# A low-rank product in fp32 column tiles from the unnormalised input, and the decay products two value blocks later

## The chip, the cores and the metric

The kernel runs on one core of one Trainium2 chip. The metric is its device time in microseconds, the median of several executions. The core has TensorE (PE: matmul, and PEld: its weight loads), VectorE (DVE), ScalarE (ACT), GpSimd (POOL) and SyncE (SP), which issues DMAs. Each engine works through its own instructions in order and waits on semaphores for the others.

## What is computed

Two transformer-like blocks on 512 tokens of width 1024, in fp32: the first with a recurrent layer, an attention layer and two MLPs, the second with gated linear attention (GLA), a pooling branch and a gated MLP. The change lies at the seam: the end of the first block's second MLP, its last norm, and the first projections of the second block.

```
x = rms_norm(x, final_norm_g)                 # end of the first block
h = rmsnorm(x, norm_mix)                      # second block
q, k, v, r, lr_f, lr_b, u, g_a, g_b = split(h @ w_in)      # lr_f, lr_b: 16 columns each
log_a_f = log_sigmoid(lr_f @ w_decay_up_fwd + b_decay_fwd) / 16
log_a_b = log_sigmoid(lr_b @ w_decay_up_bwd + b_decay_bwd) / 16
b = cumsum(log_a)   (in chunks of 64 tokens)
q_e, k_e, k_d = q * exp(b), k * exp(-b), k * exp(b_last - b)
scores = mask(q_e @ k_e^T);  o = scores @ v + q_e @ state;  kv = k_d^T @ v
```

There are 4 heads; q and k have 128 columns a head, v has 256.

## The kernel before

**Data.** The activations stand turned, as X: 8 chunks k of 128 features, each 128 x 512 tokens, in fp32. For the large products an operand is split into a high part (rounded to fp32r) and a low part (the rest): Ahi and Alo are X times the norm weights gfm, split so. A product of 128 output features (helper `product`, with `three`) runs over 8 chunks, three fp32r matmuls each (lines 1023 to 1025: hi by hi, hi by lo, lo by hi), 24 matmuls of 512 tokens in all. The tokens' reciprocal roots are not in Ahi: they come from a separate sum of squares and are multiplied in as a result leaves its bank (`scale_out`, line 2105).

**Weights.** They come in units of 8 chunks x 256 columns. SyncE loads a unit into one of two stages, ScalarE rounds it into whi (`hi`, line 1500), and VectorE takes the difference into wlo (`lo`, line 2093). `take_unit` makes TensorE wait for the latter. Both engines do this at fixed places between their other steps. The unit "lr" holds the 32 low-rank columns three times beside each other. It and K0 use the same slot of whi and wlo, Q0 and V0 the other; then V1 uses K0's, and Q1 V0's.

**PSUM.** Six banks go round as a ring in the order of the labels added to it: `begin` waits until the bank's last user has been read. Banks 6 and 7 are apart.

**The order of TensorE** is written by hand. After the last turned sums of the MLP (line 1160) it runs: the low-rank product lr (96 columns) and qk 0 beside each other chunk by chunk (`first_products`, in the order TURN = 4, 5, 6, 7, 0, 1, 2, 3, as Ahi and Alo become ready); qk 2; qk 1 (unit K0); the two root sums over the squares (fp32 with ones, lines 1330 and 1331); qk 3; the values of head 0 (unit V0) in four blocks of 128 tokens, 24 matmuls of 256 columns each, with the decay products z (line 1339) behind the first; the values of head 1 (V1); the scores and turned keys of head 0 (lines 1359 and 1059); qk 4 and qk 6 (unit Q1), and so on: states (1375), r 0, outputs (1385, 1393).

**The others around it.** ScalarE squares each chunk twice (line 1819), and splits K0's hi between the fourth and the fifth pair. GpSimd and VectorE sum the squares (938, 2601); VectorE takes K0's lo behind its third sum. Then come V0's split and the roots; the reciprocal (2611); lr scaled and split into lr3 by rows (high, low, high parts in the three copies, against the same of wdec); the scaling of qk 0 to 3; V1's split. The decays of head 0 go from z through Abs, Exp and Ln on ScalarE (1842, 1845, 1848), two scans on VectorE, Exp (1854) and products for the scaled queries and keys. Behind that chain, in ScalarE's order, stand the copies of V of head 0 out of its banks (1871, 1873) and the hi of Q1; in VectorE's stands Q1's lo. After it follow on VectorE a reciprocal, eight steps on X, the masked scores, R0's lo and the scaling of qk 4.

Of the kernel before, what the change touches and what calls it, by code (L numbers as in the profile page):

```python
# [9 lines left out]
ALU = mybir.AluOpType  # L10
# [77 lines left out]
def program(nc, I, out, scratch):  # L88
# [62 lines left out]
    ysum = const("ysum", [128, 8])  # L151
    dec = at("dec", o_const + 4 * KB + 512, [128, 2, 8])
# [96 lines left out]
    unit("lr", *[wpiece(win, 0, 8, 3072, 32, 32 * i) for i in range(3)])  # L249
# [174 lines left out]
    pair("lr", "lr")  # L424
    ring.add(("qk", 0))
    pair(("Q", 0), ("qk", 2))
    pair(("K", 0), ("qk", 1), ("qk", 3))
    ring.add(("v", 0, 0), ("z", 0, 0), ("z", 0, 1))
    pair(("V", 0), ("v", 0, 1))
# [156 lines left out]
    V = pool("V", 16, [128, 4, 4, 256])  # L586
    lr, lr3 = pool("lr", 96, [96, S]), pool("lr3", 32, [96, S], R)
    CM = pool("CM", 34, [128, 8, 64])
    wdec, wdec3 = pool("wdec", 102, [96, 2, 512]), pool("wdec3", 36, [96, 2, 512], R)
    SR = pool("SR", 48, [128, 8, S])  # L590
# [420 lines left out]
    def tensor_program(e):  # L1011
# [25 lines left out]
        def first_products(fill, *parts):  # L1037


            for i, k in enumerate(TURN):  # L1040
                e.wait_ge(s_alo, FILL[fill] + i + 1)
                for label, s, c0_, width in parts:
                    ps = begin(label) if i == 0 else ring.bank(label)
                    t = three(ps[0:width, :], hi_of(s)[:, k, c0_:c0_ + width], lo_of(s)[:, k, c0_:c0_ + width], Ahi[:, k, :], Alo[:, k, :], i == 0, i == 7)
                    if i == 7:
                        t.then_inc(*ring.put(label))
# [274 lines left out]

        s = take_unit("lr")
        first_products("gla", ("lr", s, 0, 96), (("qk", 0), take_unit(("Q", 0)), 0, 128))
        s = u_of["Q", 0]
        product(("qk", 2), s, 128, Ahi, Alo)
        s = take_unit(("K", 0))
        product(("qk", 1), s, 0, Ahi, Alo)
        e.wait_ge(s_tsp, 7)
# [3 lines left out]
        product(("qk", 3), s, 128, Ahi, Alo)  # L1332
# [8 lines left out]
        def values(h, behind_first=None):  # L1341
            s = take_unit(("V", h))
            for jj in range(2):
                ps = begin(("v", h, jj))
                for j in (2 * jj, 2 * jj + 1):
                    for k in range(8):
                        t = three(ps[:, (j % 2) * 256:(j % 2 + 1) * 256], Ahi[:, k, j * 128:(j + 1) * 128], Alo[:, k, j * 128:(j + 1) * 128],
                                  hi_of(s)[:, k, :], lo_of(s)[:, k, :], k == 0, k == 7)
                    if j == 0 and behind_first:
                        behind_first()  # L1350
                t.then_inc(*ring.put(("v", h, jj)))
# [130 lines left out]
    def scalar_program(e):  # L1482
        st = Steps(s_act)

        def hi(u):
# [14 lines left out]
            e.activation(hi_of(u)[:, 0:nk, 0:n], source(u), ACT.Copy).then_inc(s_hi, 1)  # L1500
# [310 lines left out]
        def for_gla(n, m):  # L1811
# [3 lines left out]
            for n, m in enumerate(TURN):  # L1815
                for i, (acc, t, kw) in enumerate(((sqa_e, sqt_e, {}), (sqb_e, sqs_e, {"scale": c1("fin1", m)}))):
                    if n > 2:
                        e.wait_ge((s_tsp, s_ssr)[i], n - 2)
                    e.activation((t[n % 2] if n else acc)[:, :], X[:, m, :], ACT.Square, **kw).then_inc(s_tsa, 1)
                if n == 3:  # L1820
                    hi(u_of["K", 0])
# [263 lines left out]
    def vector_program(e):  # L2085
        st = Steps(s_dve)

        def lo(u):
# [3 lines left out]
            e.wait_ge(s_hi, u + 1)  # L2092
            e.tensor_tensor(lo_of(u)[:, 0:nk, 0:n], source(u), f32(hi_of(u)[:, 0:nk, 0:n]), ALU.subtract).then_inc(s_lo[slot_of[u]], 1)  # L2093
# [499 lines left out]
        e.tensor_tensor(gfm[:, :], c1("fin1", 0, 8), c2("mix2", 0, 8), ALU.mult).then_inc(*st.inc())  # L2593
        mlp(1, lambda n, m: scaled_lo("gla", m, gfm[:, m:m + 1], n))
# [379 lines left out]
```

## Time and profile before

| | us |
|---|---|
| median of 3 runs | 1801.88 |
| lowest, highest | 1801.77, 1803.03 |
| the profiled execution | 1804.51 |
| its span, first to last instruction | 1803.3 |

The profile is of one execution. Its page gives the busy time of each engine and the costliest groups, its timeline the instructions in order of time, its stretches the busy time between two moments with the granted clock of TensorE (1.00 is 2.4 GHz). A matmul's record is longer than its share of the pipeline: full products follow each other every 0.23 us with records of 0.39, so the starts are to be read. An fp32 matmul leaves two records, and rows of one kind may be merged.

### The profile page before, as it was taken

What the parts mean: (1) busy time and instruction counts of PE and PEld (TensorE: products, weight loads), DVE (VectorE), ACT (ScalarE), POOL (GpSimd) and SP (SyncE); (2) the same over time, 40 slices, a digit from 0 to 9 for tenths busy, and PEclk for the clock granted to TensorE, in tenths of its full rate; (3) what the DMA queues carried; (4) which work ended last, traced back from release to release, by engine and by line L of the source; (5) the groups of instructions that cost most, each with busy time, mean ns of one, the idle gap of its engine ahead of it and who ended that gap; (6) DMA issues with size and microseconds to landing.
All of it is one profiled execution on the core that took longest, in us unless ns stands there. A gap on an engine that the chain in (4) does not pass through costs nothing.

```text
span 1803.3 us, 21912 instructions
## 1 busy us (share of the span) xinstructions
PE 1787.6 (99%) x8577; PEld 1458.5 (81%) x8577; DVE 1270.5 (70%) x1680; ACT 813.0 (45%) x1072; POOL 305.8 (17%) x246
## 2 busy tenths in 40 slices
PE   9999999999999999999999999999999999999998
PEld 7888888888877668888888878888888888888886
DVE  7896868686879865767686888666446555846757
ACT  6753534343444862444343455566323343323334
POOL 0004000000145874000000041111012311011012
PEclk9999999999999999999999999999999999999999
DMA  7233253443234003452525232222332323431512
GB/s 235 94 117 117 71 187 83 130 130 102 65 100 136 29 1 117 131 173 47 167 59 172 44 110 76 66 71 71 103 107 83 104 83 140 140 117 48 175 59 76
DMA packets 153350, 186.39 MB, mean 103 GB/s; under 512 B 8704, under 2 KB 121472, under 8 KB 153248
## 3 DMA queue, kind: packets, MB, share of 16 engines
q1 hardware_dynamic: 144944, 166.13, 28.4%
q0 software_dynamic: 7760, 18.35, 4.9%
q8 instruction: 68, 1.11, 0.2%
q10 hardware_dynamic: 544, 0.52, 0.1%
q14 instruction: 34, 0.28, 0.0%
HBM read 182.71 MB, written 2.14 MB: 103 GB/s over the span
## 4 chain that ended last, share of the span: by engine, by line
PE 86%; DVE 7%; ACT 3%; POOL 2%; issue 1%; DMA 1%; SPq 0%; DVEq 0%; POOLq 0%; ACTq 0%
PE bank L1023 27%; PE bank L1024 26%; PE bank L1025 26%; PE bank L1244 1%; PE bank L1059 1%; DVE work L2495 1%; PE bank L1270 1%; DVE t L2492 1%; DVE XC L2190 1%; PE bank L1375 1%; ACT whi L1500 1%; DVE wlo L2093 1%; PE bank L1393 1%; PE bank L1248 1%; DVE work L2470 0%
## 5 line engine op out<-in xcount | busy, mean ns | idle before, releaser
L1023 PE MATMUL bank<-Ahi,whi 128*128 128x512 f32 (+1 forms) x1400 | 549.2, 392 | 0.8 <-DVE wlo L2119 0.5
L1025 PE MATMUL bank<-Ahi,wlo 128*128 128x512 f32 (+1 forms) x1400 | 544.0, 389 | 0.0
L1024 PE MATMUL bank<-Alo,whi 128*128 128x512 f32 (+1 forms) x1400 | 544.0, 389 | 0.0
L2093 DVE TENSOR_TENSOR wlo<-stage,whi 128x2048 fp32r<-128x2048 f32 (+1 forms) x133 | 304.9, 2293 | 174.3 <-ACT whi L1500 174.1
L1500 ACT ACTIVATE whi<-stage 128x2048 fp32r<-128x2048 f32 (+1 forms) x139 | 262.6, 1889 | 189.3 <-PE bank L1025 157.3
L1023 PEld LDWEIGHTS bank<-Ahi,whi 128*128 128x128 f32 x1400 | 262.8, 188 | 62.8 <-issue 8.2
L1025 PEld LDWEIGHTS bank<-Ahi,wlo 128*128 128x128 f32 x1400 | 262.7, 188 | 54.6
L1024 PEld LDWEIGHTS bank<-Alo,whi 128*128 128x128 f32 x1400 | 263.0, 188 | 54.0 <-issue 1.2
L1023 PE MATMUL bank<-whi,Hh 128*128 128x512 f32 x602 | 234.8, 390 | 0.0
L1025 PE MATMUL bank<-whi,Hl 128*128 128x512 f32 x602 | 234.2, 389 | 0.0
L1024 PE MATMUL bank<-wlo,Hh 128*128 128x512 f32 x602 | 234.2, 389 | 0.0
L1023 PEld LDWEIGHTS bank<-whi,Hh 128*128 128x128 f32 x602 | 113.0, 188 | 24.5 <-DVE wlo L2093 0.6
L1025 PEld LDWEIGHTS bank<-whi,Hl 128*128 128x128 f32 x602 | 113.0, 188 | 23.5
L1024 PEld LDWEIGHTS bank<-wlo,Hh 128*128 128x128 f32 x602 | 113.0, 188 | 23.3
L1650 ACT ACTIVATE Hw<-ht 128x512 f32<-128x512 f32 x64 | 40.5, 633 | 201.2 <-DVE ht L2295 201.2
L2093 DVE TENSOR_TENSOR wlo<-quad,whi 128x2048 fp32r<-128x2048 f32 (+1 forms) x44 | 98.6, 2241 | 30.1 <-ACT whi L1500 30.1
L1500 ACT ACTIVATE whi<-quad 128x2048 fp32r<-128x2048 f32 (+1 forms) x44 | 82.3, 1871 | 72.7 <-DVE quad L2336 49.2
L816 POOL DMA_DIRECT2D quad<-in_mlp_w_down x8 | 10.5, 1316 | 535.8 <-DVE quad L2336 498.5
L2356 DVE TENSOR_TENSOR D<-D,bank 128x512 f32<-128x512 f32 x138 | 90.4, 682 | 14.3 <-PE bank L1025 14.1
L2295 DVE SCALAR_TENSOR_TENSOR ht<-bank,rstd 128x512 f32<-128x512 f32 x64 | 44.0, 688 | 62.2 <-PE bank L1025 61.2
L1002 POOL TENSOR_TENSOR Hw<-fu,fg 128x512 f32<-128x512 f32 x22 | 28.4, 1291 | 286.4 <-DVE fu L2851 286.4
L926 POOL TENSOR_SCALAR pt<-pt,stat 128x128 f32<-128x128 f32 (+3 forms) x60 | 63.3, 1066 | 14.4 <-DVE stat L2532 13.6
(364 smaller groups left out, 2491.3 us busy)
## 6 DMA issues: line engine op xcount, KB each, us to landing
stage<-in_mlp_w_up SPq DMA_DIRECT2D x32, 1024.0 KB, 5.3
stage<-in_w_in SPq DMA_DIRECT2D x22, 1024.0 KB, 5.1
stage<-in_w_ffn_in SPq DMA_DIRECT2D x22, 1024.0 KB, 4.9
quad<-in_mlp_w_down SPq DMA_DIRECT2D x16, 1024.0 KB, 6.6
stage<-in_mlp_w_down SPq DMA_DIRECT2D x16, 1024.0 KB, 5.1
quad<-in_mlp_w_down POOLq DMA_DIRECT2D x8, 1024.0 KB, 8.6
stage<-in_rec_w_in SPq DMA_DIRECT2D x6, 1024.0 KB, 5.2
stage<-in_att_w_in SPq DMA_DIRECT2D x6, 1024.0 KB, 5.1
```

The costliest lines, as they stand in the source:

```text
L926: e.tensor_scalar(p, p, stat[:, i % 8, 2:3], None, ALU.mult).then_inc(s_p, 1)
L1002: e.tensor_tensor(to, fu[n % 2][:, :].rearrange("p (a t) -> p a t", a=2), fg[n % 4][:, :].rearrange("p (a t) -> p a t", a=2), ALU.mult).th ...
L1023: e.matmul(ps, hi, rh, start=first, stop=False, skip_group_check=onto)
L1024: e.matmul(ps, hi, rl, start=False, stop=False, skip_group_check=onto)
L1025: return e.matmul(ps, lo, rh, start=False, stop=last, skip_group_check=onto)
L1059: t = e.transpose(ps[:, i * 128:(i + 1) * 128], part, ident_[:, :])
L1244: x = e.matmul(ps[:, 0:nk], QT[p0:p0 + 64, h // 2, j * 128:(j + 1) * 128], KT[p0:p0 + 64, h // 2, 0:nk], start=True, stop=not j)
L1500: e.activation(hi_of(u)[:, 0:nk, 0:n], source(u), ACT.Copy).then_inc(s_hi, 1)
L1650: e.activation(to, x, ACT.Square).then_inc(s_q, 1)
L2093: e.tensor_tensor(lo_of(u)[:, 0:nk, 0:n], source(u), f32(hi_of(u)[:, 0:nk, 0:n]), ALU.subtract).then_inc(s_lo[slot_of[u]], 1)
L2295: e.scalar_tensor_tensor(ht[n % 8][:, :], ring.bank(label)[:, :], 0.0, rstd[:, :], ALU.max, ALU.mult).then_inc(*ring.take(label))
L2356: e.tensor_tensor(to, to, ps[:, :], ALU.add if SIGN[r] > 0 else ALU.subtract).then_inc(*done)
```

## The change

The unit "lr" is loaded once, 32 columns. ScalarE copies it, unrounded, into low_w, which lies where whi of its slot lies, and VectorE multiplies it there by gfm. A constant sel (128 x 96: four identities of 32 above each other, three times beside each other) is made on VectorE before the second MLP.

TensorE multiplies low_w with the raw X in plain fp32: 8 matmuls of 32 columns, one a chunk, in two groups of four. Chunk k writes partitions 32 (k mod 4) on of the bank "lrp", so four chunks go to four column tiles; the second group adds to the first. The first group stands before, the second in the middle of the first products, which now are qk 0 and qk 2. ScalarE copies lrp to SBUF (lrs) behind its second pair of squares. The matmul sel by lrs adds the four parts and lays the sum out three times, as "lr" was; its place is behind the root sums, which themselves now stand behind qk 3. The decay products z stand behind the third value block of head 0. The ring's order follows, with one label more.

```diff
-    unit("lr", *[wpiece(win, 0, 8, 3072, 32, 32 * i) for i in range(3)])
+    unit("lr", wpiece(win, 0, 8, 3072, 32))
...
-    pair("lr", "lr")
-    ring.add(("qk", 0))
-    pair(("Q", 0), ("qk", 2))
+    pair("lr", "lrp")
+    pair(("Q", 0), ("qk", 0), ("qk", 2))
     pair(("K", 0), ("qk", 1), ("qk", 3))
-    ring.add(("v", 0, 0), ("z", 0, 0), ("z", 0, 1))
-    pair(("V", 0), ("v", 0, 1))
+    ring.add("lr")
+    pair(("V", 0), ("v", 0, 0), ("v", 0, 1))
+    ring.add(("z", 0, 0), ("z", 0, 1))
...
+                if i == 4 and between:
+                    between()
...
-        s = take_unit("lr")
-        first_products("gla", ("lr", s, 0, 96), (("qk", 0), take_unit(("Q", 0)), 0, 128))
-        s = u_of["Q", 0]
-        product(("qk", 2), s, 128, Ahi, Alo)
+        take_unit("lr")
+        low_ps = begin("lrp")
+        def low_rank(*ks):
+            for k in ks:
+                e.wait_ge(*ring.free(("xt", 1, k)))
+                row = k % 4 * 32
+                t = e.matmul(low_ps[row:row + 32, :], low_w[:, k, 0:32], X[:, k, :], start=k >= 4, stop=k < 4)
+            if ks[-1] == TURN[-1]:
+                t.then_inc(*ring.put("lrp"))
+        low_rank(*TURN[:4])
+        s = take_unit(("Q", 0))
+        first_products("gla", (("qk", 0), s, 0, 128), (("qk", 2), s, 128, 128), between=lambda: low_rank(*TURN[4:]))
         s = take_unit(("K", 0))
         product(("qk", 1), s, 0, Ahi, Alo)
+        product(("qk", 3), s, 128, Ahi, Alo)
...
-        product(("qk", 3), s, 128, Ahi, Alo)
+        ps = begin("lr")
+        e.wait_ge(*ring.free("lrp"))
+        e.matmul(ps[0:96, :], sel[:, :], lrs[:, :], start=True, stop=True).then_inc(*ring.put("lr"))
...
-                    if j == 0 and behind_first:
-                        behind_first()
+                    if j == 2 and behind_third:
+                        behind_third()
...
+                if n == 1:
+                    e.wait_ge(*ring.full("lrp"))
+                    e.activation(lrs[:, :], ring.bank("lrp")[:, :], ACT.Copy).then_inc(*ring.take("lrp"))
                 if n == 3:
                     hi(u_of["K", 0])
...
+                e.tensor_tensor(low_w[:, :, :], low_w[:, :, :], gfm[:, :].unsqueeze(2).broadcast_to([128, nk, n]), ALU.mult).then_inc(s_lo[slot_of[u]], 1)
```

TensorE at the start of the second block's products, before. whi_55 is the slot of "lr" and later of K0, whi_54 that of Q0; D are the MLP's sums that are turned:

```order
L1160 MATMUL bank<-ident_64,D_101 128x128 [waits s_free3]
L1023 MATMUL bank<-Ahi_50,whi_55 96x512 [waits s_alo,s_free0,s_lo0,s_lo1]
L1024 MATMUL bank<-Alo_51,whi_55 96x512
L1025 MATMUL bank<-Ahi_50,wlo_58 96x512
L1023 MATMUL bank<-Ahi_50,whi_54 128x512 [waits s_free1]
L1024 MATMUL bank<-Alo_51,whi_54 128x512
```

The same place now:

```order
L1166 MATMUL bank<-ident_64,D_102 128x128 [waits s_free3]
L1337 MATMUL bank<-X_49,low_w_198 32x512 [waits s_free4,s_free0,s_lo1]
L1337 MATMUL bank<-X_49,low_w_198 32x512 [waits s_free5]
L1337 MATMUL bank<-X_49,low_w_198 32x512 [waits s_free0]
L1337 MATMUL bank<-X_49,low_w_198 32x512 [waits s_free1]
L1027 MATMUL bank<-Ahi_50,whi_54 128x512 [waits s_free1,s_alo,s_lo0]
```

Of each chunk's six matmuls the three of 96 columns have gone from between those of Q0, and four of 32 columns stand ahead.

TensorE from the end of qk 3 to the values of head 0, where before the root sums stood ahead of qk 3:

```order
L1029 MATMUL bank<-Ahi_50,wlo_58 128x512
L1349 MATMUL bank<-sq_e_92,ones_66 128x512 [waits s_ssr_and_decay_low,s_tsp]
L1350 MATMUL bank<-sq_e_93,ones_66 128x512
L1353 MATMUL bank<-lrs_204,sel_80 96x512 [waits s_free0,s_free5]
L1027 MATMUL bank<-whi_54,Ahi_50 128x256 [waits s_free0,s_lo0]
```

Three fp32 products now stand between qk 3 and the values.

ScalarE from the copy of lrp to the hi of K0, now (whi_55 from stage_53 is K0's hi):

```order
L1845 ACTIVATE lrs_204<-bank 128x512 [waits s_full0]
L1842 ACTIVATE sq_e_91<-X_49 128x512
L1842 ACTIVATE sq_e_94<-X_49,cols_69 128x512
L1842 ACTIVATE sq_e_95<-X_49 128x512 [waits s_tsp]
L1842 ACTIVATE sq_e_96<-X_49,cols_69 128x512 [waits s_ssr_and_decay_low]
L1523 ACTIVATE whi_55<-stage_53 128x2048 [waits s_full0,s_load1]
```

The first of these rows is new; the squares and K0's hi follow it as they were.

## Rows read from the trace of the kernel before

**Rows 1.** The page, part 1: engine, busy us (share) and instructions.
```profile
PE 1787.6 (99%) x8577; PEld 1458.5 (81%) x8577; DVE 1270.5 (70%) x1680; ACT 813.0 (45%) x1072; POOL 305.8 (17%) x246
```

**Rows 2.** Timeline, TensorE: start, us, line, operation; "x" counts merged records.
```profile
1050.06 0.48 PE L1023 MATMUL bank<-Ahi,whi 128*96 128x512 f32 x1
...
1072.47 1.10 PE L1330 MATMUL bank<-sq_e,ones 128*128 128x512 f32 x2
1073.40 1.02 PE L1331 MATMUL bank<-sq_e,ones 128*128 128x512 f32 x2
...
1079.73 0.28 PE L1023 MATMUL bank<-whi,Ahi 128*128 128x256 f32 x1
...
1082.71 0.70 PE L1339 MATMUL bank<-lr,wdec 96*128 96x512 f32 x2
...
1103.41 1.95 PE L1359 MATMUL bank<-qe,ke 128*128 128x128 f32 x16
...
1105.98 0.47 PE L1023 MATMUL bank<-Ahi,whi 128*128 128x512 f32 x1
...
1119.13 0.50 PE L1023 MATMUL bank<-Ahi,whi 128*128 128x512 f32 x1
```

**Rows 3.** By stretch: length, busy us as in rows 1, clock, DMA share, GB/s.
```profile
1050.06:1061.27 11.21, 11.21 (x52) 8.48 (x50) 9.00 (x12) 8.32 (x14) 3.90 (x4) 1.00 0.39 113
1061.27:1066.73 5.46, 5.46 (x26) 4.50 (x24) 5.36 (x4) 3.77 (x6) 4.81 (x2) 1.00 0.03 3
...
1079.73:1082.71 2.98, 2.98 (x25) 2.85 (x24) 2.88 (x6) 1.98 (x2) 2.23 (x4) 1.00 0.02 0
```

**Rows 4.** Timeline, VectorE: sums of squares, then the lo of K0.
```profile
1058.60 4.70 DVE L2601 TENSOR_TENSOR sq_e<-sq_e,sq_e 128x512 f32<-128x512 f32 x3 [1.45 <-ACT sq_e L1819]
1063.22 2.28 DVE L2093 TENSOR_TENSOR wlo<-stage,whi 128x2048 fp32r<-128x2048 f32 x1
```

**Rows 5.** Timeline, VectorE: the lo of Q1.
```profile
1101.71 2.29 DVE L2093 TENSOR_TENSOR wlo<-stage,whi 128x2048 fp32r<-128x2048 f32 x1 [4.24 <-ACT whi L1500]
```

**Rows 6.** Timeline, TensorE: full-width products, 64-column ones, the next product.
```profile
1132.34 1.89 PE L1385 MATMUL bank<-V,sc_t 128*128 128x256 f32 x8
1134.16 3.24 PE L1393 MATMUL bank<-ST,qe 128*64 128x256 f32 x28
1137.34 0.50 PE L1023 MATMUL bank<-Ahi,whi 128*128 128x512 f32 x1
```

**Rows 7.** Timeline, ScalarE: the second pair of squares, and the hi of K0.
```profile
1057.86 0.71 ACT L1819 ACTIVATE sq_e<-X,cols 128x512 f32<-128x512 f32 x1
...
1060.82 1.92 ACT L1500 ACTIVATE whi<-stage 128x2048 fp32r<-128x2048 f32 x1
```

**Rows 8.** Timeline, VectorE: reciprocal, QK 0 and 2, lo of V1, QK 4 and 6.
```profile
1076.62 3.35 DVE L2611 RECIPROCAL rstd<-sq_e 128x512 f32<-128x512 f32 x1 [0.70 <-ACT sq_e L1832]
...
1080.62 1.27 DVE L2105 TENSOR_TENSOR QK<-bank,rstd 128x512 f32<-128x512 f32 x2
...
1084.93 2.23 DVE L2093 TENSOR_TENSOR wlo<-stage,whi 128x2048 fp32r<-128x2048 f32 x1
...
1116.60 1.28 DVE L2105 TENSOR_TENSOR QK<-bank,rstd 128x512 f32<-128x512 f32 x2
```

**Rows 9.** Timeline, ScalarE: Abs of z, end of v 0 0, hi of Q1.
```profile
1083.22 1.26 ACT L1842 ACTIVATE t<-bank,negb 128x512 f32<-128x512 f32 x2
...
1098.54 0.47 ACT L1873 ACTIVATE V<-bank,rtok 128x256 f32<-128x256 f32 x1
...
1099.78 1.90 ACT L1500 ACTIVATE whi<-stage 128x2048 fp32r<-128x2048 f32 x1
```

**Rows 10.** Busy time by stretch, around 520 us, as in rows 3.
```profile
518.00:520.00 2.00, 1.55 (x8) 1.38 (x8) 0.00 (x0) 0.30 (x1) 2.00 (x1) 0.50 0.00 0
...
526.00:528.00 2.00, 2.00 (x14) 2.00 (x13) 1.09 (x3) 0.00 (x0) 0.00 (x0) 1.00 0.00 0
```

**Rows 11.** Timeline, TensorE, around 518 us.
```profile
518.45 2.14 PE L1197 MATMUL bank<-kk,qi 64*128 64x256 f32 x8 [1.32 <-DMA kk<-kk]
```

More of the change, by code:

```diff
@@ L151, in program @@
     ysum = const("ysum", [128, 8])
+    sel = const("sel", [128, 96])
+    assert c_at[0] <= o_const + 4 * KB + 512
     dec = at("dec", o_const + 4 * KB + 512, [128, 2, 8])
@@ L586, in program @@
     V = pool("V", 16, [128, 4, 4, 256])
+    low_w = at("low_w", o_whi + slot_of[u_of["lr"]] * 8 * KB, [128, 8, 32])
     lr, lr3 = pool("lr", 96, [96, S]), pool("lr3", 32, [96, S], R)
@@ L589, in program @@
     wdec, wdec3 = pool("wdec", 102, [96, 2, 512]), pool("wdec3", 36, [96, 2, 512], R)
+    lrs = pool("lrs", 56, [128, S])
     SR = pool("SR", 48, [128, 8, S])
@@ L1035, in product, with first_products @@
             i.then_inc(*ring.put(label))
-        def first_products(fill, *parts):
+        def first_products(fill, *parts, between=None):
             for i, k in enumerate(TURN):
+                if i == 4 and between:
+                    between()
                 e.wait_ge(s_alo, FILL[fill] + i + 1)
@@ L1339, in decays, with values @@
                 e.matmul(ps[:, :], wdec3[:, d, h * 128:(h + 1) * 128], lr3[:, :], start=True, stop=True).then_inc(*ring.put(("z", h, d)))
-        def values(h, behind_first=None):
+        def values(h, behind_third=None):
             s = take_unit(("V", h))
@@ L1499, in hi @@
                 e.wait_ge(*used(behind[u]))
-            e.activation(hi_of(u)[:, 0:nk, 0:n], source(u), ACT.Copy).then_inc(s_hi, 1)
+            to = low_w[:, :, :] if u == u_of["lr"] else hi_of(u)[:, 0:nk, 0:n]
+            e.activation(to, source(u), ACT.Copy).then_inc(s_hi, 1)
         def scaled_hi(m, gc):
@@ L2092, in lo @@
             e.wait_ge(s_hi, u + 1)
+            if u == u_of["lr"]:
+                e.wait_ge(*gfm_there)
+                e.tensor_tensor(low_w[:, :, :], low_w[:, :, :], gfm[:, :].unsqueeze(2).broadcast_to([128, nk, n]), ALU.mult).then_inc(s_lo[slot_of[u]], 1)
+                return
             e.tensor_tensor(lo_of(u)[:, 0:nk, 0:n], source(u), f32(hi_of(u)[:, 0:nk, 0:n]), ALU.subtract).then_inc(s_lo[slot_of[u]], 1)
@@ L2593, in vector_program @@
         e.tensor_tensor(gfm[:, :], c1("fin1", 0, 8), c2("mix2", 0, 8), ALU.mult).then_inc(*st.inc())
+        gfm_there = st.now()
+        e.tensor_tensor(sel[:, 32:96], ident[:, 0:64], ident[:, 64:128], ALU.add).then_inc(*st.inc())
+        e.wait_ge(*st.now())
+        e.tensor_tensor(sel[:, 0:32], sel[:, 32:64], sel[:, 64:96], ALU.add).then_inc(*st.inc())
+        e.wait_ge(*st.now())
+        for i in (1, 2):
+            e.tensor_copy(sel[:, 32 * i:32 * i + 32], sel[:, 0:32]).then_inc(*st.inc())
         mlp(1, lambda n, m: scaled_lo("gla", m, gfm[:, m:m + 1], n))
```

## The prediction

> **What bounds the kernel now.** The page's first part comes first: TensorE is busy for 1787.6 us, 99% of the span [rows 1]. So a microsecond counts only if TensorE gets it or waits for it, and the argument is about the 70 us in which the second block's first projections run. There I read TensorE's timeline for the starts of its stages [rows 2], the stretches between them for the price of a product [rows 3], and ScalarE's and VectorE's timelines for when each thing that TensorE needs is ready. What the reader is to see: TensorE hardly waits here, but two of its supplies arrive with little to spare. The split of weight unit K0 (hi on ScalarE, lo on VectorE) ends at 1063.22 + 2.28 = 1065.50 [rows 4], and TensorE takes it 72 products after 1050.06, at 11.21 + 5.46 us, 1066.73 [rows 2, 3]: slack 1.2 us. The split of Q1 ends at 1101.71 + 2.29 = 1104.00 [rows 5] and is taken at 1105.98 [rows 2]: slack 2.0 us. Q1's split stands on both engines behind the whole chain that the decay product z starts. The change shortens TensorE's way to the first and moves z nearer to the second.
>
> **The removed product.** The low-rank product is 24 products of 96 columns. Before, 48 interleaved ones take 11.21 us and 24 of qk 2 take 5.46 [rows 3]; after, qk 0 and qk 2 are the 48 interleaved ones, so 5.46 us go.
>
> **The added products.** Eight fp32 products of 32 columns on the raw X, in two groups of four. One fp32 product of 512 takes 0.93 us, from the start of line 1330 to that of line 1331 [rows 2]. Four column tiles beside each other are not in this trace, so I bound them: one after another 8 x 0.93 = 7.4 us, fully beside each other 2 x 0.93 = 1.9. Nearest are the 14 fp32 products of 64 columns of line 1393 (two records each): 3.18 us from their start to the next product, 0.23 us each, where the 4 of full width on line 1385 take 1.82 / 4 = 0.455 each [rows 6]. Two tiles do run beside each other, at twice the rate and with different moving operands. I take 1.0 us a group, 2.0 in all. The product after them starts a tenth of a microsecond late [rows 6], which is in that. The adding product with sel is one more fp32 product of 512: 0.93 us. By work alone: -5.46 + 2.0 + 0.93 = -2.5 us. The four small steps that make sel, and load, hi and scaling of low_w, lie on VectorE, SyncE and ScalarE well ahead of need, hidden by the second layer's last products: nothing.
>
> **First wait: K0.** TensorE wants K0 at 1050.06 + 1.0 + 5.6 + 1.0 + 5.6 = 1063.3 now. The split isn't earlier, it is later: on ScalarE the new copy of lrp stands behind the second pair of squares (start 1057.86 [rows 7]; the second group ends near 1057.9, so the copy waits for nothing) and costs 0.6 us, a copy of that size. So K0's hi starts at 1061.4 instead of 1060.82 and ends at 1063.3 [rows 7]. VectorE's three sums, 4.70 us from 1058.60 [rows 4], are fed by those squares and end near 1063.6; K0's lo then runs to 1065.85. TensorE stands still for 2.5 us, and qk 1 starts at 1065.9 instead of 1066.73. Behind it nothing of the 2.5 us gained is left but 0.8. The groups could cost 2.5 us more and this start would hardly move.
>
> **To the first value block.** 48 products by 5.46 / 24 make 10.9: 1076.8. The two root sums are no longer ahead of qk 3 but behind it. Before, they start at 1072.47 [rows 2]. Now they start at 1076.8, +4.4 us; with sel, 3 x 0.93 = 2.8 us, the values start at 1079.65, where they started at 1079.73: -0.1 us. What is new is that all that hangs on the root is 4.4 us late: the reciprocal ends at 1076.62 + 3.35 + 4.4 = 1084.35 instead of 1079.97 [rows 8]. QK 0 is scaled behind lr (0.6 us) and frees its bank at about 1085.7. By the new ring of banks the second half of the values (v 0 1) takes just that bank, and TensorE is there after two blocks, 2 x 2.88 = 5.76 us (a block is the stretch of 2.98 [rows 3] less the tenth in which z waits), at 1085.4: 0.3 us of waiting. The split of V1, from 1084.93 [rows 8], comes 4.4 us later too, ending near 1091.5; it is taken at 1092.0, so it is just hidden.
>
> **Second wait: the decays.** z was issued behind one value block, at 1082.71 [rows 2]; now it is behind three: 1079.65 + 8.64 + 0.3 = 1088.6, 5.9 us later. From z a chain leads through ScalarE and VectorE without slack: Abs at 1083.22, Exp, Ln, the scans, the factors, then V 0's two halves scaled and freed (the first half's second copy starts at 1098.54), hi of Q1 at 1099.78 [rows 9], lo of Q1 until 1104.00 [rows 5]; 21.3 us from z to split. All of it moves by 5.9 us. TensorE's own work moves by 0.1: it would be at the scores at 1103.55. Two things are late there. First, the scores' first bank is now the one of v 0 0, freed at 1098.54 + 0.47 + 5.9 = 1104.9: 1.4 us of waiting. Then the scores and the turned keys take 1105.98 - 1103.41 = 2.6 us [rows 2], to 1107.6, and Q1's split ends at 1104.00 + 5.9 = 1109.9: 2.4 us. qk 4 starts at 1110.0 instead of 1105.98, +4.0 us. The size doesn't hang on the first of these two, since the second ends last.
>
> **What follows.** VectorE is 5.9 us late and TensorE 4.0. QK 4 is scaled from 1116.60 [rows 8], so its bank is free at 1117.2 + 5.9 = 1123.1; the product r 0, at 1119.13 [rows 2] + 4.0 = 1123.1, takes it: at most 0.1 us more. From there VectorE waits for TensorE again, and TensorE is gap-free, so the 4 us stay to the end. Sum: -2.5 (work) + 2.5 (K0) + 0.3 + 1.4 + 2.4 (banks, Q1) - 0.1 = +4.0 us. The execution profiled took 1804.51 us for a span of 1803.3; it was 2.6 us above the median of 1801.88, and 1808.5 would be its counterpart. Against the median: **1805.9 us**. With half a microsecond to either side for K0's split, for z's chain and for the noise of the runs, its own range is 1804.7 to 1807.3.
>
> **Rival 1: the clock falls.** Ahead of 518 us TensorE did small transposes, one fp32 product and then waited 1.32 us at 518.45; the stretch from 518 has a granted clock of 0.50, 1.2 GHz, and at 526 it is 1.00 again [rows 10, 11]. Two places after the change look similar: 2.5 us of standing at 1063, and 1.4 and 2.4 us around short work at 1103 to 1110. For it: that row. Against: around both places stand full products, where ahead of 518 us there were hardly any. The low clock lasted about 7 us, with products at half rate: +3.4 us on +4.0, 1809.3 us. The Trainium skill (TensorE: Matmul & The Clock Gate, Part 1) says that inactivity throttles the array and activity releases it; by that rule this is what a long enough wait does, and [rows 10] agree.
>
> **Rival 2: the four tiles don't overlap.** Then a group takes 3.7 us. The second ends near 1063.2, ScalarE's copy waits for it, and squares, sums and both steps of K0 follow: split at about 1070.9, 5 us behind my 1065.9. All behind moves by that: 1810.9 us. Against it: the rate of line 1393 [rows 6]. The Trainium skill (TensorEngine Tiling, Key Properties) says that a change of tiling mode drains the array; the product at 1137.34 takes 0.50 us [rows 6], a small drain, and it would lie in front of K0's wait anyway.
>
> **Rival 3, not slower: K0 is there in time.** If the squares and sums give K0's split by 1063.3 (VectorE's sums take 1.6 us each beside GpSimd's own; alone they could be shorter), the root starts at 1074.2, z at 1086.0, and Q1's split at 1107.3 ends the wait: +1.4, 1803.3 us, within 0.2%. It decides from 1.0 us on: if K0 comes at 1064.9, the total is 1804.9. Against: hi of K0 can't end before 1063.3 by ScalarE's own order [rows 7], so lo can't before 1065.5. The same size of result comes if z's chain has slack that I don't see.
>
> **Rival 4, faster: neither wait is there.** The gain of 2.5 stays: 1799.3 us. It needs the chain from z to Q1 to shrink from 21.3 to 17.5 us or less [rows 2, 5]; nothing in it is idle long enough.
>
> **How the numbers follow.** Forecast 0.58, rival 1 0.14, rival 2 and other ways to lose more 0.07, rival 3 and its kin (from 1801.5 to 1804.7) 0.18, rival 4 0.03. The range from 1802.3 to 1809.6 leaves out rival 4, the low end of rival 3 and rival 2, some 0.15. 0.2%, about what a measurement can tell from no change, is 3.6 us: the border lies at 1805.5, inside the forecast's own range, whose upper two thirds lie above it (0.38). Slower: 0.38 + 0.14 + 0.07 = 0.59; within: 0.20 + 0.18 = 0.38; faster: 0.03.
>
> **What would show it.** K0: qk 1's first product waits for VectorE's wlo, some 2.5 us, and starts 0.8 us earlier than before relative to the stage's start. The groups: eight 32-column products with group starts 0.9 to 1.1 us apart. Values start where they did. z 5.9 us later. qk 4's first product waits for wlo, and the scores for ScalarE's V. If qk 4 starts less than 2 us later than before, the second wait is wrong; if the stage before K0 shows no gap, the first is. A granted clock under 1.00 at 1063 to 1073 or 1107 to 1117 speaks for rival 1. The forecast fails if K0's split ends ahead of 1064.9, or if the stage loses or regains time behind 1123.

## The result, and the profile after

| | before | after |
|---|---|---|
| median of 13 runs each, us | 1802.95 | 1808.21 |
| lowest, highest | 1801.57, 1804.89 | 1805.88, 1809.98 |
| the profiled execution | 1804.51 | 1807.09 |
| its span | 1803.3 | 1805.9 |

After takes 1.003 of before's time, 95% interval 1.0023 to 1.0037: +5.3 us, slower. The range from 1802.3 to 1809.6 us and the likeliest sign of the prediction hold; its forecast was +4.0 us. As an absolute time 1808.21 us lies above the forecast's own range, which ended at 1807.3; before's median over these 13 runs is itself 1.1 us above the 1801.88 that the forecast started from.

The spans differ by 2.6 us only, because of something far ahead of the change: around 518 us before's profiled execution has the low clock of [rows 10], and after's has not. This stretch of after answers to [rows 10]; the columns are length, busy us of PE, PEld, DVE, ACT and POOL, granted clock, DMA share and GB/s:

```profile
518.00:520.00 2.00, 1.47 (x10) 1.14 (x11) 0.00 (x0) 0.64 (x2) 2.00 (x1) 1.00 0.00 0
```

Of the twelve kernels traced here six have a low clock there and six have not, some built on before and some on after in each half. In one series of 27 runs of before, the 11 with a mean granted clock of 0.999 took 1801.20 to 1802.05 us and the 10 with 0.997 took 1804.14 to 1805.10. So I compare traces from the last work in front of the change that they share, the 13 turned sums of the MLP, to the end of the span. TensorE's timeline of before has them here (start, us, line, operation; in brackets the idle time ahead and who ended it):

```profile
1048.66 1.64 PE L1160 MATMUL bank<-ident,D 128*128 128x128 f32 x13 [0.58 <-DVE D L2356]
```

From there before takes 1803.3 - 1048.66 = 754.6 us. After starts them at 1045.83 and takes 1805.9 - 1045.83 = 760.1: **+5.4 us since the turned sums**, which is what the medians say too. All experiments below are given in that unit as well. It is read from one execution of each kernel, so where the medians say something else, that is given too. TensorE's last product of all, in before, in after and in the kernel before with only z moved (an experiment below):

```profile
1795.45 0.39 PE L1025 MATMUL bank<-whi,Hl 128*128 128x512 f32 x1
```
```profile
1797.72 0.39 PE L1029 MATMUL bank<-whi,Hl 128*128 128x512 f32 x1
```
```profile
1798.27 0.39 PE L1025 MATMUL bank<-whi,Hl 128*128 128x512 f32 x1
```

It starts 1795.45 - 1048.66 = 746.79 us after the turned sums in before, 751.89 in after: on TensorE the loss is 5.1 us. The other 0.3 lie behind its last product, where the last norms and writes take 8.18 us instead of 7.85. This end takes 7.5 to 7.9 us in the traces of the three kernels built on before and 8.1 to 8.2 in the nine built on after; why is open.

TensorE's timeline of after, with the rows that answer to [rows 2], and the waits:

```profile
1045.83 1.64 PE L1166 MATMUL bank<-ident,D 128*128 128x128 f32 x13 [0.59 <-DVE D L2386]
1047.40 1.07 PE L1337 MATMUL bank<-X,low_w 128*32 128x512 f32 x8
...
1054.28 1.07 PE L1337 MATMUL bank<-X,low_w 128*32 128x512 f32 x8
1055.28 0.50 PE L1027 MATMUL bank<-Ahi,whi 128*128 128x512 f32 x1
...
1062.72 0.50 PE L1027 MATMUL bank<-Ahi,whi 128*128 128x512 f32 x1 [1.70 <-DVE wlo L2123]
...
1073.73 1.02 PE L1349 MATMUL bank<-sq_e,ones 128*128 128x512 f32 x2
1074.59 1.02 PE L1350 MATMUL bank<-sq_e,ones 128*128 128x512 f32 x2
1075.45 1.02 PE L1353 MATMUL bank<-lrs,sel 128*96 128x512 f32 x2
...
1082.43 0.39 PE L1027 MATMUL bank<-whi,Ahi 128*128 128x256 f32 x1 [0.22 <-DVE QK L2135]
...
1085.40 0.63 PE L1361 MATMUL bank<-lr,wdec 96*128 96x512 f32 x2
...
1101.69 2.05 PE L1381 MATMUL bank<-qe,ke 128*128 128x128 f32 x16 [1.27 <-ACT V L1899]
1103.57 1.04 PE L1065 MATMUL bank<-ident,t 128*128 128x128 f32 x8
1106.68 0.60 PE L1027 MATMUL bank<-Ahi,whi 128*128 128x512 f32 x1 [2.07 <-DVE wlo L2123]
1107.08 0.63 PE L1028 MATMUL bank<-Alo,whi 128*128 128x512 f32 x1
1107.51 0.63 PE L1029 MATMUL bank<-Ahi,wlo 128*128 128x512 f32 x1
...
1121.43 0.50 PE L1027 MATMUL bank<-Ahi,whi 128*128 128x512 f32 x1
```

The reader sees the four waits that the prediction named, at the places it named: on VectorE's wlo for qk 1 (K0's split), on a scaled QK for v 0 1, on ScalarE's V for the scores, on wlo again for qk 4 (Q1's split). A group of four 32-column products takes 1.00 us (1054.28 to 1055.28). And a fifth thing stands at the end: behind qk 4's first product the next ones follow 0.40 to 0.43 us apart with records of 0.63, not 0.23 apart. The stretches of after show why, in the clock behind POOL's column:

```profile
1100.00:1106.68 6.68, 3.34 (x28) 2.90 (x26) 2.44 (x3) 6.42 (x12) 2.46 (x2) 1.00 0.01 1
1106.68:1110.00 3.32, 3.32 (x8) 2.61 (x9) 3.28 (x2) 2.14 (x2) 0.00 (x0) 0.54 0.64 182
1110.00:1119.38 9.38, 9.38 (x41) 7.46 (x39) 9.28 (x18) 0.00 (x0) 0.00 (x0) 0.98 0.14 49
```

TensorE is busy for 3.34 of 6.68 us up to qk 4; then for some 3.4 us it is granted 1.2 instead of 2.4 GHz, and does in them the work of 1.7. Behind K0's wait, with full products on both sides, the clock stayed at 1.00:

```profile
1062.00:1073.00 11.00, 10.28 (x45) 8.54 (x46) 9.37 (x6) 5.86 (x7) 10.37 (x7) 1.00 0.34 99
```

On VectorE's timeline the three sums of squares and K0's lo, the rows that answer to [rows 4], and on ScalarE's the copy of lrp and K0's hi:

```profile
1055.77 1.28 DVE L2638 TENSOR_TENSOR sq_e<-sq_e,sq_e 128x512 f32<-128x512 f32 x1 [1.44 <-ACT sq_e L1842]
1057.38 3.08 DVE L2638 TENSOR_TENSOR sq_e<-sq_e,sq_e 128x512 f32<-128x512 f32 x2 [0.34 <-ACT sq_e L1842]
1060.39 2.28 DVE L2123 TENSOR_TENSOR wlo<-stage,whi 128x2048 fp32r<-128x2048 f32 x1
```
```profile
1055.64 0.57 ACT L1845 ACTIVATE lrs<-bank 128x512 f32<-128x512 f32 x1
...
1058.39 1.90 ACT L1523 ACTIVATE whi<-stage 128x2048 fp32r<-128x2048 f32 x1
```

Lo starts 1060.39 - 1055.77 = 4.62 us behind the first sum, in before 1063.22 - 1058.60 = 4.62 [rows 4]. Hi ends at 1060.29, just ahead of lo, where before it ended at 1062.74 [rows 7], half a microsecond ahead: the copy has taken the slack that hi had, and has cost lo nothing. The later squares did reach VectorE, which stands 0.34 us behind its first sum; but that first sum took 1.28 us, where in before the three take 4.62 / 3 = 1.54 each. TensorE is busy for 1785.2 us, 2.4 less than in [rows 1], in a span that is longer from the change on:

```profile
PE 1785.2 (99%) x8571; PEld 1454.7 (81%) x8571; DVE 1270.4 (70%) x1684; ACT 812.7 (45%) x1073; POOL 305.5 (17%) x246
```

### The profile page after: what moved, and what is told of

The parts are those of the page before. It is cut to its first block, busy times and chain, and to the rows that moved or that the text cites. A ratio compares the mean times of both kernels' runs of the same rounds, so it can differ in the third digit from the quotient of the medians.

```text
span 1805.9 us, 21905 instructions
## 1 busy us (share of the span) xinstructions
PE 1785.2 (99%) x8571; PEld 1454.7 (81%) x8571; DVE 1270.4 (70%) x1684; ACT 812.7 (45%) x1073; POOL 305.5 (17%) x246
## 4 chain that ended last, share of the span: by engine, by line
PE 85%; DVE 8%; ACT 3%; issue 2%; POOL 2%; DMA 0%; DVEq 0%; POOLq 0%; ACTq 0%
PE bank L1027 26%; PE bank L1028 26%; PE bank L1029 26%; PE bank L1250 1%; PE bank L1065 1%; DVE work L2525 1%; PE bank L1276 1%; DVE t L2522 1%; DVE wlo L2123 1%; DVE XC L2220 1%; PE bank L1397 1%; ACT whi L1523 1%; PE bank L1415 1%; PE bank L1254 1%; DVE work L2500 0%
## 5 line engine op out<-in xcount | busy, mean ns | idle before, releaser
L930 POOL TENSOR_SCALAR pt<-pt,stat 128x128 f32<-128x128 f32 (+3 forms) x60 | 63.4, 1068 | 14.2 <-DVE stat L2562 13.5
```

The source lines that it names most:

```text
L930: e.tensor_scalar(p, p, stat[:, i % 8, 2:3], None, ALU.mult).then_inc(s_p, 1)
```

## The experiments

The theory: the change takes 2.7 us of work from TensorE, and pays for it at two supplies that became late, K0's split and, through z's place, Q1's split with V's copies ahead of it; the low clock comes on top. The rivals: the four column tiles cost what is lost; or z's place alone makes the whole loss and the rest is neutral; or the clock is the cause and not an addition. Each ratio is against before, run on the same chip between the others (its medians lay at 1802.71 to 1803.20), with 11 runs of each kernel, 5 of the one with one tile.

### Q1's split earlier

After, with ScalarE's hi of Q1 moved ahead of the scaled keys' second part and both copies of V 0:

```diff
         decay_factors(0)
+        hi(u_of["V", 1] + 1)
         remaining(0)
         copy_v(0)
-        hi(u_of["V", 1] + 1)
         copy_v(1)
```

> The changed kernel with one step moved: ScalarE takes the hi of Q1 behind the decay factors, in the 2.1 us in which it waits for VectorE, instead of behind the copies of V. Theory (Q1's split is what TensorE waits for at qk 4, 2.07 us, and that wait brings the low clock of about 1.6 us behind it): the split ends near 1102.4 on the changed kernel's own time scale, no wait at qk 4, no low clock behind it, 3.0 to 3.7 us faster than the changed kernel, so 1.5 to 2.3 us over the kernel before (ratio 1.0010). Rival (the wait at qk 4 is for something else, the bank of v 1 0 or the turned keys): it stays, and so does the time, 1.003. Rival (the clock falls because of the wait at the scores, 1.27 us, or of both together): the low clock stays, and only 2.1 us are gained, 1.0018.

Measured: 1805.57 us, ratio 1.0011 (1.0002 to 1.0020); +2.1 us since the turned sums, 3.3 less than after. TensorE's timeline and the stretch behind it:

```profile
1101.72 2.05 PE L1381 MATMUL bank<-qe,ke 128*128 128x128 f32 x16 [1.28 <-ACT V L1899]
1103.61 0.60 PE L1065 MATMUL bank<-ident,t 128*128 128x128 f32 x4
1104.60 0.66 PE L1065 MATMUL bank<-ident,t 128*128 128x128 f32 x4 [0.39 <-POOL t L965]
1105.01 0.47 PE L1027 MATMUL bank<-Ahi,whi 128*128 128x512 f32 x1
```
```profile
1104.00:1110.00 6.00, 5.61 (x28) 4.56 (x27) 5.96 (x6) 3.24 (x4) 0.54 (x1) 1.00 0.56 178
```

The wait of 2.07 us is gone, and the wait for V stays as it was, 1.28 us. A new one of 0.39 us comes in the middle of the turned keys, which wait for GpSimd's product t, and that waits for ScalarE's Exp in `remaining`, which now stands behind hi. The clock stays at 1.00. From the turned keys to qk 4 it is now 1105.01 - 1103.61 = 1.4 us, for 3.1 in after and 0.8 in before. So qk 4 starts 1.7 us earlier, and with the low clock's 1.6 that makes the 3.3 us; by the medians it is 2.9. In these two traces the low clock comes and goes with this wait, and not with the one of 1.28 us. The split itself ended at 1103.41, a microsecond later than expected, because VectorE's lo took 3.36 us instead of 2.28 with GpSimd's two products running beside it; that was still ahead of need.

### K0's split earlier

After, with K0's hi behind the copy of lrp and its lo behind VectorE's first sum:

```diff
-                if n == 3:
                     hi(u_of["K", 0])
...
-            if m == 3:
+            if m == 1:
                 lo(u_of["K", 0])
```

> The changed kernel with K0's hi behind ScalarE's copy of lrp and its lo behind VectorE's first sum, two pairs of squares earlier. Theory (the split of K0 is the whole wait of 1.70 us at qk 1): no wait there, root sums, z and qk 4 all 1.7 us earlier, since the sums of squares still end ahead of the roots; 1.7 us faster than the changed kernel, 3.6 us over the kernel before (ratio 1.0020). Rival (the sums of squares come late now and hold the roots): the wait moves from qk 1 to the roots and nothing is gained, 1.003. Rival (the decay chain's late places are fixed to something that K0 does not move): z earlier, qk 4 not.

Measured: 1805.42 us, ratio 1.0013 (1.0004 to 1.0022); +3.5 us since the turned sums, 1.9 less than after. The waits of TensorE from 1045 to 1125 us (us in total, times, longest; the two largest of four) no longer hold qk 1's:

```profile
PE bank L1027 <- DVE wlo L2122: 2.1, 1, 2.1
PE bank L1381 <- ACT V L1898: 1.3, 1, 1.3
```

and the low clock stands behind qk 4 as in after, here in two stretches of three us:

```profile
1107.00:1110.00 3.00, 2.10 (x7) 1.68 (x8) 3.00 (x2) 3.00 (x4) 0.00 (x0) 0.79 0.26 57
1110.00:1113.00 3.00, 3.00 (x10) 2.39 (x9) 2.96 (x4) 0.04 (x1) 0.00 (x0) 0.65 0.87 298
```

So K0's wait is worth 1.9 us in the trace, a little more than the 1.70 that it shows, and the low clock doesn't come from it: it is there without it. (The medians give 3.0 us for this edit, +2.2 over before; more on that under the filled wait.) The sums of squares now end near 1073.7, 1.2 us ahead of the root sums that need them; that is the slack of this place.

### Both

> The changed kernel with both steps moved. Theory: the two waits are apart and add: 1.7 and 3.0 to 3.7 us, to 0.5 us over down to 0.1 us under the kernel before (ratio 1.0000). What is left against the sum of the work (-2.5 us) are the waits at the scores for V's bank (1.3 us) and at v 0 1 (0.2 us). Rival (one wait hides behind the other): no more than the larger of the two single gains, 1.0010.

Both edits together: 1802.28 us, ratio 1.0001 (0.9992 to 1.0010); +0.2 us since the turned sums. The waits for V (1.28 us), for GpSimd's t (0.39) and for QK (0.22) stay, and the clock is 1.00. The two splits and what hangs on them, the low clock too, are thus 5.2 of the 5.4 us. The saving of work and the waits that are left nearly cancel.

### Before, with z behind the third value block

```diff
-    ring.add(("v", 0, 0), ("z", 0, 0), ("z", 0, 1))
-    pair(("V", 0), ("v", 0, 1))
+    pair(("V", 0), ("v", 0, 0), ("v", 0, 1))
+    ring.add(("z", 0, 0), ("z", 0, 1))
...
-                    if j == 0 and behind_first:
+                    if j == 2 and behind_first:
```

> The kernel before with only the decay products (and their banks) moved behind the third value block. Theory (z's place is what makes Q1's split late): z at 5.6 us later, the scores wait 1.2 us for V's bank, qk 4 waits for Q1's split and starts 3.7 us later than before, with the low clock behind it 1.5 us more: +3.7 to +5.3 us, ratio 1.0021 to 1.0029. That is nearly the whole loss, since the rest of the change then gains nothing net. Rival (the loss comes from the late root, not from z's place): under +1.5 us, 1.0008.

Measured: 1806.97 us, ratio 1.0022 (1.0013 to 1.0031); +5.0 us since the turned sums. This one part, without any change of the low-rank product, makes nearly the whole loss in the trace; by the medians it is +3.8 of +5.3 us. TensorE's waits and its clock behind them:

```profile
PE bank L1023 <- DVE wlo L2093: 2.1, 1, 2.1
PE bank L1359 <- ACT V L1873: 1.3, 1, 1.3
...
PE bank L1330 <- DVE sq_e L2601: 0.3, 1, 0.3
```
```profile
1107.00:1110.00 3.00, 2.83 (x8) 2.22 (x8) 3.00 (x2) 2.31 (x3) 0.00 (x0) 0.60 0.51 132
```

The waits for wlo and V are after's, 2.07 and 1.27 us, to the hundredth: so they go by the chain from z to Q1's split and by the number of products between z and the scores, not by when z starts. It also has the low clock. So what the rest of the change adds on top is 5.4 - 5.0 = +0.4 us; at TensorE's last product it is 751.89 - 752.12 = -0.2 us, and by the medians +1.5. None of the three shows that the shorter product gains anything much here: K0's wait eats most of what it saves.

### After, with z behind the second value block

```diff
-    pair(("V", 0), ("v", 0, 0), ("v", 0, 1))
-    ring.add(("z", 0, 0), ("z", 0, 1))
+    ring.add(("v", 0, 0), ("z", 0, 0), ("z", 0, 1))
+    pair(("V", 0), ("v", 0, 1))
...
-                    if j == 2 and behind_third:
-                        behind_third()
                 t.then_inc(*ring.put(("v", h, jj)))
+                if jj == 0 and behind_third:
+                    behind_third()
```

> The changed kernel with z behind the second value block instead of the third. Theory (the chain from z to Q1's split is rigid, 21.3 us): z waits about 1.4 us for the low part of lr, goes out 1.6 us earlier than in the changed kernel, and the scores and qk 4 come 1.6 us earlier, with the wait at the scores gone or small; 1.6 us faster, up to 3 if the low clock goes too: 2.3 to 3.7 us over the kernel before, ratio 1.0013 to 1.0020. Rival (z's place saves a wait as large as what it costs): no difference from the changed kernel, 1.003.

Measured: 1804.40 us, ratio 1.0011 (1.0002 to 1.0020); +2.5 us since the turned sums. The waits:

```profile
PE bank L1027 <- DVE wlo L2123: 2.2, 2, 1.7
PE bank L1361 <- DVE lr L2654: 1.6, 1, 1.6
```

Here z can't start at its place: lr, scaled by the root, is 1.57 us late, since the roots stand behind qk 3. TensorE pays that at z instead of 1.27 at the scores, and keeps 0.49 of the 2.07 at qk 4; the clock is 1.00. So the third block is too late for z and the second too early, as long as the roots are where they are; the better of the two is the second, by 2.9 us in the trace and 4.0 in the medians.

### The product in one column tile

After, but all eight 32-column products write partitions 0 to 31, so none has another beside it; the copy and sel use 32 rows:

```diff
-                row = k % 4 * 32
-                t = e.matmul(low_ps[row:row + 32, :], low_w[:, k, 0:32], X[:, k, :], start=k >= 4, stop=k < 4)
+                t = e.matmul(low_ps[0:32, :], low_w[:, k, 0:32], X[:, k, :], start=k == TURN[0], stop=k == TURN[-1])
...
-        e.matmul(ps[0:96, :], sel[:, :], lrs[:, :], start=True, stop=True).then_inc(*ring.put("lr"))
+        e.matmul(ps[0:96, :], sel[0:32, :], lrs[0:32, :], start=True, stop=True).then_inc(*ring.put("lr"))
...
-                    e.activation(lrs[:, :], ring.bank("lrp")[:, :], ACT.Copy).then_inc(*ring.take("lrp"))
+                    e.activation(lrs[0:32, :], ring.bank("lrp")[0:32, :], ACT.Copy).then_inc(*ring.take("lrp"))
```

> The changed kernel with all eight 32-column products in one column tile, one after another, summed there (the adding product then takes 32 rows of lrs). It prices what lying beside each other saves. Theory (four tiles run beside each other): a group of four takes 3.4 to 3.7 us here instead of 1.0; ScalarE's copy of lrp waits some 4 us, K0's split is that much later, and everything behind it: 4 to 5 us over the changed kernel, 9.5 over the kernel before, ratio 1.0053. Rival (small products cost their columns, tiles or not): a group stays near 1.0 us and the time that of the changed kernel.

Measured: 1811.71 us, ratio 1.0049 (1.0035 to 1.0062); +10.1 us since the turned sums. TensorE's timeline:

```profile
1047.57 3.62 PE L1336 MATMUL bank<-X,low_w 128*32 128x512 f32 x8
1051.12 0.50 PE L1027 MATMUL bank<-Ahi,whi 128*128 128x512 f32 x1
...
1056.78 3.62 PE L1336 MATMUL bank<-X,low_w 128*32 128x512 f32 x8
1060.33 0.50 PE L1027 MATMUL bank<-Ahi,whi 128*128 128x512 f32 x1
```

A group takes 1051.12 - 1047.57 = 3.55 us instead of 1.00. The four column tiles run beside each other, 3.5 times as fast; what rival 2 said would follow if they didn't is real, and its price was about right (3.7 us a group, +9.0 us in all, against +8.6 in the medians and +10.1 in the trace, where the low clock adds its part; these are five runs). K0's wait is still 1.42 us, behind 5.1 us more of products. ScalarE's timeline tells why:

```profile
1060.44 0.59 ACT L1844 ACTIVATE lrs<-bank 32x512 f32<-32x512 f32 x1 [4.53 <-PE bank L1336]
```

The copy of lrp stands 4.53 us for the second group, with the later squares and K0's hi behind it, so the split moves along with that group: qk 1 starts 1067.48 - 1046.00 = 21.5 us after the turned sums, for 16.9 in after. Work in front of a wait is not free when the awaited chain starts behind that work.

### Before, with Q1's split earlier

The first edit, in before:

> The kernel before with only ScalarE's hi of Q1 moved into its wait behind the decay factors. Theory: there Q1's split was ready 2.0 us ahead of need, so nothing changes: ratio 1.0000, within 0.0005. Rival (the early split helps in other ways, by VectorE's later work coming sooner): faster by 1 us or more, and then part of q1_early's gain is not the wait's.

Measured: 1803.48 us, ratio 1.0000 (0.9992 to 1.0009); -0.3 us since the turned sums. Where nothing waits for the split, moving it does nothing that can be measured, so the gain in the first experiment is the wait's and not that of a better order on ScalarE.

### The wait filled

After, with eight unused products of 512 tokens into bank 6 ahead of qk 4; they take the place of idle time and add work that nobody reads:

```diff
             if h == 0:
+                for i in range(8):
+                    e.matmul(banks[6][:, :], Ahi[:, 0, 0:128], Ahi[:, 0, :], start=True, stop=True)
                 s = take_unit(("Q", 1))
```

> The changed kernel with eight further fp32r products of 512 (1.8 us, their result is not used) on TensorE ahead of qk 4, where it otherwise waits 2.07 us for Q1's split. They tell the wait from the low clock that follows it. Theory (the array's standing idle there is what lowers the clock): qk 4 starts when it did, at 1.00, the low clock of 3.4 us behind it is gone, 1.6 us faster than the changed kernel, +3.6 us, ratio 1.0020. Rival (the low clock comes from the stage's small products and scores, or from chance): it stays, ratio 1.003 or more, since the filling saves nothing.

Measured: 1808.10 us, ratio 1.0025 (1.0016 to 1.0034); +4.0 us since the turned sums. TensorE's timeline, and the stretches behind qk 4's start:

```profile
1107.02 2.07 PE L1431 MATMUL bank<-Ahi 128*128 128x512 f32 x8
...
1109.34 0.50 PE L1027 MATMUL bank<-Ahi,whi 128*128 128x512 f32 x1 [0.24 <-DVE wlo L2125]
```
```profile
1108.00:1110.00 2.00, 1.75 (x8) 1.13 (x7) 2.00 (x2) 1.97 (x5) 0.00 (x0) 1.00 0.00 0
1110.00:1112.00 2.00, 2.00 (x10) 1.61 (x9) 2.00 (x1) 1.48 (x1) 0.00 (x0) 1.00 0.70 194
```

qk 4 starts 1109.34 - 1048.45 = 60.89 us after the turned sums, in after 60.85: the split is what it waits for. With the wait filled the clock stays at 1.00, and the trace ends 1.4 us shorter than after's. In the profiled executions the picture is uniform: the four kernels with the wait of 2.07 us (after, K0 earlier, z third in before, one tile) all have some 3.4 us of low clock behind it, and the other eight kernels traced, before among them, have none there. Three of these eight (Q1's split earlier, both, the wait filled) keep the wait of 1.27 us for V. The timed runs don't bear the 1.4 us out: by the medians the filled kernel is 5.4 us over before and after 5.3, and the filled kernel's interval holds both what was expected, 1.0020, and the rival's 1.003. So that the standing idle lowers the clock is shown by the traces alone, and what it costs in the median is not. The runs of the kernel with K0's split earlier point to a possible reason: its fastest four of eleven, 1803.46 to 1803.98, are some 2.1 us above the fastest of before beside it, 1801.41, where its trace gives +3.5 with the low clock and about +1.9 without. So some executions seem to be spared it. How many, I can't say from medians.

### Three waits at once

After, with Q1's and K0's splits early, z behind the second block, and the root sums moved into qk 3, behind its fifth chunk:

```diff
-        product(("qk", 3), s, 128, Ahi, Alo)
-        e.wait_ge(s_tsp, 7)
...
+        ps = begin(("qk", 3))
+        for k in range(8):
+            if k == 5:
+                e.wait_ge(s_tsp, 7)
...
+            t = three(ps[:, :], hi_of(s)[:, k, 128:256], lo_of(s)[:, k, 128:256], Ahi[:, k, :], Alo[:, k, :], k == 0, k == 7)
+        t.then_inc(*ring.put(("qk", 3)))
```

> The changed kernel with K0's and Q1's splits early, the root sums behind the fifth chunk of qk 3 instead of behind all eight, and z behind the second value block. Theory: nothing waits between the first products and qk 4 but some 0.5 us at the roots for the sums of squares, so the gain of the work comes out: 5.5 us removed, 2.0 + 0.9 added, -2.0 to -2.6 us, ratio 0.9987. Rival (the four tiles or the added product cost time elsewhere that no wait shows): 1.0000 or more.

Measured: 1801.91 us, ratio 0.9993 (0.9984 to 1.0002); -1.3 us since the turned sums. That is less than expected, and the interval still holds 1. One wait is left, at the root sums:

```profile
1072.47 1.10 PE L1351 MATMUL bank<-sq_e,ones 128*128 128x512 f32 x2 [0.85 <-DVE sq_e L2641]
```

VectorE did K0's lo ahead of its sums, and so ends those later than the earlier roots want them. The last kernel puts K0's hi behind the third pair of squares (`n == 2`) and its lo behind the second sum (`m == 2`):

> As all_three, but K0's hi and lo stand behind the third pair of squares and the second sum (one place later). In all_three the sums of squares end 1.2 us later than in the changed kernel and hold the roots for 0.84 us. Theory: the sums end some 0.8 us earlier, the roots wait for nothing, qk 1 waits at most 0.4 us for K0, and 0.3 to 0.7 us are gained on all_three: -1.6 to -2.0 us against the kernel before, ratio 0.9990. Rival (the sums are as slow wherever K0's split stands): the wait at the roots stays and the one at qk 1 is added, ratio 0.9995 or more.

Measured: 1800.53 us, ratio 0.9990 (0.9982 to 0.9999); -1.6 us since the turned sums. TensorE's waits from 1045 to 1125 us, all of them:

```profile
PE bank L1166 <- DVE D L2390: 0.6, 1, 0.6
PE bank L1027 <- DVE wlo L2127: 0.5, 1, 0.5
```

The first is before's too. This version beats both kernels, before by some 2 us (2.2 in the medians, 1.6 in the trace), with an interval that just leaves out 1. It keeps the column tiles and the raw X, so it isn't these that cost the time; the saving shows once what hangs behind it is early enough.

## Why the prediction came out right, step by step

**The work.** Forecast -2.5 us, measured about -2.7: a group is 1.00 us as taken from [rows 6], and an fp32 product takes 0.86 us (1074.59 - 1073.73), not the 0.93 of [rows 2], three times. The 0.93 was the price of a product behind a wait: in before the root sums start 1072.47 - 1071.94 = 0.53 us behind the last product of qk 1, where 0.23 would do, and two other traces put this down to VectorE's sums. These 0.3 us of waiting, which the prediction didn't have, are gone in after. Small costs stand against both. The first product starts 0.17 us later behind the turned sums than before (1.57 us for 1.40), and the two runs of 24 products behind the groups take 5.88 and 5.58 us, where the forecast had 5.6 for each.

**K0.** Forecast a wait of 2.5 us, measured 1.70. The failed step is "VectorE's three sums are fed by those squares and end near 1063.6", 0.4 us later than in before: the copy of lrp moved K0's hi but not the sums, and hi had just as much slack as the copy took. (The shorter first sum is part of what rival 3 considered, that VectorE's sums "could be shorter" alone; here it was worth those 0.4 us and not the 2.5.) TensorE's last product ahead of the wait also came some 0.2 us later than the sum said (1060.63, so that the next was due at 1060.86, 13.5 us after the first product instead of 13.2). Qk 1 starts 1062.72 - 1047.40 = 15.3 us after the first product, for 15.8 forecast and 16.7 before. This step was mis-sized by 0.5 in the start and by 0.8 in the wait; its place, its cause and its sign held, and removing it gave 1.9 us back in the trace. One sentence of this step is wrong: "The groups could cost 2.5 us more and this start would hardly move." In one tile the two groups cost 5.1 us more and the start moved by 4.6, since the copy of lrp waits for the second group.

**Up to the values.** Forecast -0.1 us, measured -0.8 (1075.45 + 0.86 is 28.9 us after the first product, 1079.73 in before was 29.7): 0.5 of it is K0's difference again, and 0.2 the fp32 products. The wait for v 0 1's bank was 0.22 for 0.3.

**The decays.** z came 5.35 us later, 38.00 against 32.65 us after the first product, for 5.9: K0's 0.5 us again. The waits that follow were 1.27 for 1.4 and 2.07 for 2.4. qk 4 starts 1106.68 - 1047.40 = 59.28 us after the first product, where before it was 55.92: +3.4 for +4.0. That z's place alone gives these waits was shown in before itself (+5.0 us in the trace with the clock's part).

**An idle time costs more than it shows.** The waits in brackets count from the end of the last record, and records are longer than the spacing of products. K0's wait of 1.70 us stands between starts at 1060.63 and 1062.72, 2.09 us where 0.23 would do, and the product after the wait holds up the next by 0.1: about 2.0 us in all. At qk 4 the turned keys' start to qk 4's start is 3.11 us, 0.79 before: 2.3 us for the 2.07 shown. So the four waits, 5.3 us as shown, cost about 6.2. With the work of -2.7 that gives the +3.5 us at qk 4 since the turned sums. The prediction worked from starts and so had this in it.

**The clock.** Here is what the forecast lacked. It gave rival 1 a chance of 0.14 with +3.4 us; what the trace shows is the same mechanism, half as long: 3.4 us at 1.2 GHz, 1.6 us lost between qk 4 and r 0. It was the second of the two places named, around short work; at the first, between full products, nothing fell. By the Trainium skill (TensorE: Matmul & The Clock Gate, Part 1) inactivity throttles the array and activity brings it back; this trace agrees at qk 4, with 0.54 behind 3.3 us of idle time in 6.7, and doesn't contradict it at K0. By the prediction's own sign, a granted clock under 1.00 behind qk 4, this is rival 1. r 0 then starts 1121.43 - 1045.83 = 75.60 us after the turned sums, 70.47 before: +5.1, and at TensorE's last product it is still +5.1.

**The sum.** +4.0 was forecast without the low clock. The trace has +3.5 at qk 4, 1.6 from the low clock and 0.3 behind TensorE's last product. Without the low clock it would have been some +3.8, so what the forecast added up was right, and to 0.2 us by luck: the wait for K0 was put too high by 0.8 in itself (0.5 in qk 1's start), and the 0.3 us at the end weren't in the sum. What failed is the clock's place in it: the rival treated as an alternative was an addition to the forecast. The forecast's own range, up to +5.4 us over 1801.88, just holds the difference of +5.3, and only with nothing to spare. Rival 2 is refuted as a description of this change (3.55 us a group only in one tile), rivals 3 and 4 by the waits that are there. Rival 4's condition, a chain shorter by 3.8 us, can't be met by itself, but one hi moved by two steps took the wait at qk 4 away.

**What stays open.** How often an execution has the low clock behind qk 4, and so what it costs in the median; and why the end behind TensorE's last product is some 0.3 us longer in the kernels built on after. The best version is 2.0 us ahead of before at TensorE's last product (1791.90 - 1047.07 = 744.83 for 746.79): some 2.7 us of saved work and the 0.3 us at the root sums, less 0.8 for its wait at qk 1 and 0.4 to 0.5 for the later first product and the longer run behind the first group.

## What to carry to other kernels

Before moving a step behind other work on the busiest engine, follow its results through every engine to the next thing that engine will wait for: here, in the traces, z's two value blocks cost twice what the shorter product saved. A weight split that stands at a fixed place between other steps is a supply with a date of its own; when the consumer gets faster, move the date with it. And where a wait surrounds short work, look at the clock behind it and price that in the same sum, rather than treating it as another case.

## What the runs showed of the hardware

- Four fp32 products of 32 columns in four column tiles take 1.00 us for 512 tokens each, with different moving operands; in one tile they take 3.55 us. The first full-width product behind them holds up the next by about a tenth of a microsecond (its record is 0.50 instead of 0.39), as it does behind a wait.
- fp32 products of 512 tokens at full width follow each other every 0.86 us, 0.93 where the first of them stood waiting; fp32r ones every 0.23.
- In all four traces that have them, the granted clock went from 1.00 to 0.50 for some 3.4 us behind waits of 1.27 and 2.07 us with short products between them. It stayed at 1.00 behind a single wait of 1.70 us between full products, and behind waits of 1.28 and 0.39 us around the same short products. Eight unused products in the second wait kept it at 1.00 in the profiled execution. In the trace of after the low clock cost 1.6 us, half of what the one at 518 us was put at; the medians leave its cost open.
- The waits behind z's chain repeat to a hundredth of a microsecond in kernels that differ in all that stands ahead of z.
